# The head norm of a gated DeltaNet layer, computed inside the recurrence's stage with tokens on partitions

## The chip, the cores and the metric

The kernel runs as one program on one core of one Trainium2 chip. The metric is the device time of one execution in microseconds (us), smaller being better. The profiled execution gives, beside that time, a span: from the first to the last instruction that the profiler recorded. All times inside the kernel are counted from the start of the span. Engine names: PE is TensorE (matmuls), PEld its weight loads, DVE VectorE, ACT ScalarE, POOL GpSimd, SP SyncE, which issues the DMAs.

## What is computed

The reference is a stack of two transformer-like blocks over 16 + 512 tokens of width 1024. The change touches its first layer, a gated DeltaNet (GDN) with 16 value heads and 8 query/key heads of 128 features. Cut to what matters:

```python
def step(state, xs):                       # one chunk of tokens, all heads
    u_c, w_c, q_c, k_c, attn_c, last_c = xs
    v_new = u_c - einsum('bhck,bhkv->bhcv', w_c, state)
    o = einsum('bhck,bhkv->bhcv', q_c, state) + einsum('bhij,bhjv->bhiv', attn_c, v_new)
    state = state * last_c[..., None, None] + einsum('bhck,bhcv->bhkv', k_c, v_new)
    return state, o
...
def rms_norm(x, w):                        # over the 128 features of one head and token
    return x * lax.rsqrt(mean(x * x, axis=-1, keepdims=True) + 1e-6) * w
...
o = rms_norm(o, w_norm) * silu(z)          # the head norm, then the gate
return o.reshape(b, t, GDN_V_DIM) @ w_out  # 2048 -> 1024
```

## The kernel before

The program is a row of stages, each closed by a barrier over all engines. Four of them matter here. `gdn_front` projects the input and prepares the recurrence (up to about 356 us). `gdn_back` runs the recurrence (356 to 563.6 us). `head_norm` normalizes the 16 heads (563.6 to 589.7 us). `gated_down` (name `gdn_out`) gates the heads with silu(z) and multiplies by `w_out` (589.7 to about 703 us).

**gdn_back.** Its work is cut into 20 units, one for each of 5 chunks (16 tokens, then four of 128) and each of 4 groups of 4 heads. A hand-written order strings them into slots t = -1, 0, 1, ..., and every engine has its own function `step(t, real, level)` that lists what it does in slot t, for units at different distances: unit t+1 is prepared, unit t reads the old state, unit t-1 gets its new values, unit t-2 updates the state and gives its output, and unit t-3 is copied out. In slots 0 to 15 (`level`) the engines also build the inverse of a triangular matrix for unit t, blockwise: `turn5`, `open5`, `close5` on PE with `copy5` on ACT and `corner5` on DVE, then `open6`, `close6` with `copy6` and `corner6`. In slots 0 to 7 DVE has `second_half` besides: transposes of 32x32 blocks in slots 0, 1, 6 and 7 and 15 elimination steps in each of slots 2 to 5. The engines run their lists in order and meet at semaphores.

PE in slot t runs `turn5`, `old_values(t)`, `open5`, `new_values(t-1)`, `close5`, `prepare(t+1)`, `open6`, `update(t-2)`, `output(t-2)`, `close6`. All eight PSUM banks are in use, one for each purpose: `vb` holds the transposed values of `prepare`, `ob` the outputs. `output(u)` multiplies with features on PSUM's partitions (state or new values stationary, decayed queries or attention moving) and waits until `outputs(u-1)` on ACT has copied `ob` into the tile `wide` (`o_done`). `open6` waits for `corner5` (`y5_done`).

The chain that carries a slot to the next off PE goes from `differ(t+1)` on DVE (L1879) over a mask on POOL (L1658) and an exponential on ACT (L1803, `weights`) to `attention(t+1)` on DVE (L1868, L1873).

**head_norm.** For each of the 16 heads, 528 tokens wide: a square on POOL (L874), a sum over the features by a matmul with ones (L886), a logarithm and an exponential on ACT (L896, L903) and the product with gain on DVE (L916).

**gated_down.** ACT and DVE split the first two weight units into a high and a low part (`split_hi`, `split_lo`, L154 and L161), then each head: silu of z (L2055), product (L2079), high part (L2058), low part (L2074), and PE multiplies as soon as the low part is there. SP first issues the 1 MB weight unit that `gdn_back` has not loaded, then the z tiles, three ahead.

Of the kernel before, what the change touches and what calls it, by code (L numbers as in the profile page):

```python
# [16 lines left out]
F32 = mybir.dt.float32  # L17
# [131 lines left out]
def split_hi(k, act, u, slot, used):  # L149

    act.wait_ge(k.raw_landed[slot], landed_value(u, slot))
    if used is not None:
        act.wait_ge(k.tile_full, used)
    k.nc.scalar.copy(k.whi[:, slot % SPLIT_SLOTS, :], k.raw[:, slot, :]).then_inc(k.hi_done, 1)  # L154


def split_lo(k, eng, u, slot):

    eng.wait_ge(k.hi_done, u + 1)
    s = slot % SPLIT_SLOTS  # L160
    eng.tensor_tensor(k.wlo[:, s, :], k.raw[:, slot, :], k.whi[:, s, :].bitcast(F32),  # L161
                      ALU.subtract).then_inc(k.lo_done, 1)
# [37 lines left out]
def unit_tiles(k, pe, u, slot, kts, xhi, xlo, first_slot, tile_free, x_ready=None):  # L200
# [4 lines left out]
    whi = k.whi[:, s, :].rearrange("p (k n) -> p k n", k=kts)  # L205
    wlo = k.wlo[:, s, :].rearrange("p (k n) -> p k n", k=kts)
# [559 lines left out]
def weight_ring(k, name, ctx):  # L766
    sb = lambda nm, shape, dt: ctx.enter_context(k.nc.sbuf_tensor(f"{name}_{nm}", shape, dt))
    k.whi, k.wlo = sb("whi", [P, SPLIT_SLOTS, UNIT], F32R), sb("wlo", [P, SPLIT_SLOTS, UNIT], F32R)
# [74 lines left out]


def head_norm(k, name, n, tile, ones, scale, gain, gain_src=None, then=(), gain_parts=()):

    nc = k.nc
    with ExitStack() as ctx:  # L850
        sb = lambda nm, shape: ctx.enter_context(nc.sbuf_tensor(f"{name}_{nm}", shape, F32))
        sq, rinv = sb("sq", [P, 4, T]), sb("rinv", [P, 4, T])
        g = sb("g", [P, n])
        sem = lambda nm: k.sem(f"{name}_{nm}")
        gain_in, squared, summed, log, inv, done = (sem(x) for x in (
            "gain_in", "squared", "summed", "log", "inv", "done"))
        gain_set = sem("gain_set")
        past4 = lambda j: not (isinstance(j, int) and j < 4)
        block = ctx.enter_context(stage(k))

        @block.sync
        def _(sp):
            if gain_src is not None:
                with nc.allow_non_contiguous_dma(reason="gains, feature on partitions"):
                    sp.dma_start(g[:, 0:gain_src.shape[1]], gain_src).then_inc(gain_in, 16)
            if then:
                load_ahead(k, sp, k.unit, then)

        @block.gpsimd
        def _(pool):  # L870
            def square(j, b):
                if past4(j):
                    pool.wait_ge(summed, j - 3)
                pool.tensor_tensor(sq[:, b, k.now], tile(j)[:, k.now], tile(j)[:, k.now], ALU.mult).then_inc(squared, 1)  # L874
            for cols, value in gain_parts:
                pool.memset(g[:, cols], value).then_inc(gain_set, 1)
            rounds(pool, n, square, 4)

        @block.tensor
        def _(pe):  # L880
            def one(j, b):
                pe.wait_ge(squared, j + 1)
                if past4(j):
                    pe.wait_ge(log, j - 3)
                for hf, half in enumerate(k.halves):
                    mm = pe.matmul(k.ps[b][:, hf, 0:k.width], ones, sq[:, b, half], start=True, stop=True)  # L886
                mm.then_inc(summed, 1)
            rounds(pe, n, one, 4)

        @block.scalar  # L890
        def _(act):
            def logarithm(j, b):
                act.wait_ge(summed, j + 1)
                if past4(j):
                    act.wait_ge(done, j - 3)
                nc.scalar.activation(parted(k, rinv[:, b, k.now]), filled(k, k.ps[b]), ACT.Ln, scale=scale,  # L896
                                     bias=k.eps[:, :])\
                    .then_inc(log, 1)
            def one(j, b):
                if not (isinstance(j, int) and j == n - 1):  # L900
                    logarithm(j + 1, (b + 1) % 4)
                act.wait_ge(log, j + 1)
                nc.scalar.activation(rinv[:, b, k.now], rinv[:, b, k.now], ACT.Exp, scale=-0.5).then_inc(inv, 1)  # L903
            nc.scalar.preload_act_table_set("natural_log_exp_and_others")
            logarithm(0, 0)
            rounds(act, n, one, 4)

        @block.vector
        def _(dve):
            if gain_src is not None:  # L910
                dve.wait_ge(gain_in, 16)
            if gain_parts:
                dve.wait_ge(gain_set, len(gain_parts))
            def one(j, b):
                dve.wait_ge(inv, j + 1)
                dve.scalar_tensor_tensor(out=tile(j)[:, k.now], in0=tile(j)[:, k.now], scalar=gain(g, j),  # L916
                                         in1=rinv[:, b, k.now], op0=ALU.mult, op1=ALU.mult).then_inc(done, 1)
            rounds(dve, n, one, 4)
# [655 lines left out]
def gdn_back(k, g, qkv, an, d, tmp, yt, yt0, out_unit):  # L1574
# [13 lines left out]
    with ExitStack() as ctx:  # L1588
# [8 lines left out]
        x5, z5, xz6 = sb("x5", [P, GRP, CH]), sb("z5", [P, GRP * 64]), sb("xz6", [P, 2, GRP * 64])  # L1597
        v_in = [k.sem(f"gdns_v{j}") for j in range(VFS)]
        names = ("masks", "diffed", "lowered", "el_exp", "eq_exp", "dt_exp", "qd_done", "kd_done", "attn_done", "kq_ready",
                 "kt_ready", "kt_done", "vt_ready", "v_done", "ks_ready", "r_done", "new_ready", "new_done", "dec_done",  # L1600
                 "su_ready", "s_done", "o_ready", "o_done", "x5_ready", "x5_done", "z5_ready", "z5_done", "y5_ready",
# [14 lines left out]
        def slots(step):  # L1616
            for t in range(-1, nun + 3):
                step(t, lambda u: 0 <= u < nun, 0 <= t < NU)

        @block.sync  # L1620
        def _(sp):
# [45 lines left out]
        def _(pe):  # L1667
            key = lambda c, kh: qkv[:, GQ + kh, first_token(c):first_token(c) + size(c)]
            def prepare(u):
# [48 lines left out]
            def output(u):  # L1718
# [48 lines left out]
            def step(t, real, level):  # L1767
                if level:
# [21 lines left out]
        def _(act):  # L1790
            out = qkv[:, 0:2 * GQ, :].rearrange("p (o q) t -> p o q t", o=2)
# [51 lines left out]
            def step(t, real, level):  # L1843
# [4 lines left out]
                if real(t - 3):  # L1848
                    outputs(t - 3)
# [4 lines left out]
                if real(t + 1):  # L1854
                    values(t + 1)
                if level:
                    copy6(t)
                if t >= 0 and real(t + 1):
                    decays(t + 1)
            slots(step)  # L1860

        @block.vector
        def _(dve):
            def attention(u):
# [74 lines left out]
            def step(t, real, level):  # L1939
                if 1 <= t <= NU:  # L1940
                    corner6(t - 1)
                if t == -1:
                    differ(0)
                if real(t):
                    attention(t)
                if real(t - 3):
                    states(t - 3)
                if real(t):
                    residual(t)
                if real(t - 1):  # L1950
                    decayed(t - 1)
                if level:
                    corner5(t)
                second_half(t)
                if t >= 0 and real(t + 1):
                    differ(t + 1)
            slots(step)
# [21 lines left out]
def gdn(k, ins):  # L1979
# [3 lines left out]
    with ExitStack() as c:  # L1983
# [4 lines left out]
        with ExitStack() as c2:  # L1988
            split_rings(k, "gdn", c2)
            weight_ring(k, "gdnf", c2)  # L1990
# [4 lines left out]
        gdn_back(k, g, qk, an, d, tmp, yt, yt0, gdn_out_unit(ins))  # L1995


def gdn_out(k, ins, then):
    qk = k.wide[:, :].rearrange("p (j t) -> p j t", t=T)
    tile = lambda j: qk[:, bass.ds(j, 1), :].rearrange("p o t -> p (o t)")  # L2000
    head_norm(k, "gdn_on", GV, tile, k.ones[:, :], 1.0 / P, lambda g, j: g[:, 0:1],
              ins["gdn_norm"].rearrange("o p -> p o"))
    k.loaded = NCH - 1
# [5 lines left out]
def gated_down(k, name, cols, gate_d, value, acc, later_gains, then=()):  # L2009
# [7 lines left out]
    u0, t0, loaded = k.unit, k.tile, k.loaded  # L2017
    with ExitStack() as ctx:
# [30 lines left out]
        def _(act):  # L2049
            split_hi(k, act, u0, ring(0), t0)  # L2050
            split_hi(k, act, u0 + 1, ring(1), t0)
# [1687 lines left out]
```

## Time and profile before

| | us |
|---|---|
| median of 3 runs (range) | 2090.13 (2087.88 to 2090.97) |
| the profiled execution | 2084.21 |
| its span | 2082.5 |
| `gdn_back` | 356 to 563.6 |
| `head_norm` and its barrier | 563.6 to 589.7 |
| `gated_down`, until PE's first matmul | 589.7 to 599.4 |

The profiled execution is 5.9 us faster than the median of the others, so a sum that is made against its rows is added to the median for a forecast. A difference of 0.2% is 4.2 us.

### The profile page before, as it was taken

To read this page: it belongs to the slowest core of one execution; us is meant where nothing else is said; L and a number is where in the kernel's file an instruction comes from. 1 tells how busy PE (TensorE), PEld (TensorE's weight loads), DVE (VectorE), ACT (ScalarE), POOL (GpSimd) and SP (SyncE) were. 2 spreads that over 40 slices of the span, in tenths; PEclk is the share of its full clock that TensorE was granted. 3 is DMA by queue.
4 is the path that set the end of the run, shared out by engine and by line. 5 is a ranking of instruction groups with operands and counts; after the bars stand their busy time and mean duration, and the time that the engine had idled before them with its cause. 6 is when DMAs were issued, how large, how long until landed. Compare 5 with 4: busy or idle time off the path is not lost. (4 is left out here: it accounts for less than half of the span.)

```text
span 2082.5 us, 31710 instructions
## 1 busy us (share of the span) xinstructions
PE 1940.6 (93%) x12868; PEld 1735.1 (83%) x12868; DVE 1079.6 (52%) x1770; ACT 860.6 (41%) x1380; POOL 171.5 (8%) x190
## 2 busy tenths in 40 slices
PE   7999998999869999999989987899999998899988
PEld 6999998889769999999989965678888885787666
DVE  6657667675583344344444156544444447852243
ACT  6557742355572342233334244443332333424442
POOL 0001221022320000000000011000000002000101
PEclk9999999589989999999999999999999998999989
DMA  7223351113253222323223322223223222311101
GB/s 179 90 73 123 119 164 42 41 42 79 64 144 102 74 90 87 96 82 100 81 62 92 95 58 65 81 81 101 91 91 101 96 86 63 122 55 47 41 1 41
DMA packets 205246, 173.91 MB, mean 84 GB/s; under 512 B 41232, under 2 KB 180496, under 8 KB 205128
## 3 DMA queue, kind: packets, MB, share of 16 engines
q1 hardware_dynamic: 205128, 172.25, 27.9%
q8 instruction: 84, 1.38, 0.3%
q14 instruction: 34, 0.28, 0.0%
HBM read 161.40 MB, written 10.83 MB: 83 GB/s over the span
## 5 line engine op out<-in xcount | busy, mean ns | idle before, releaser
L161 DVE TENSOR_TENSOR main_wlo<-raw,main_whi 128x2048 fp32r<-128x2048 f32 x106 | 242.9, 2292 | 363.1 <-ACT main_whi L154 363.1
L154 ACT CAST main_whi<-raw 128x2048 fp32r<-128x2048 f32 x106 | 201.6, 1903 | 413.7 <-PE ps L176 412.4
L176 PE MATMUL ps<-ffn_xhi,main_whi 128*128 128x264 f32 (+1 forms) x768 | 205.3, 322 | 6.6 <-DVE ffn_xlo L646 6.6
L176 PE MATMUL ps<-ffn_xhi,main_wlo 128*128 128x264 f32 (+1 forms) x768 | 206.0, 323 | 0.0
L176 PE MATMUL ps<-ffn_xlo,main_whi 128*128 128x264 f32 (+1 forms) x768 | 205.8, 322 | 0.0
L176 PE MATMUL ps<-ffn_ahi,main_wlo 128*128 128x264 f32 (+1 forms) x768 | 205.4, 322 | 0.0
L176 PE MATMUL ps<-ffn_alo,main_whi 128*128 128x264 f32 (+1 forms) x768 | 205.2, 321 | 0.0
L176 PE MATMUL ps<-ffn_ahi,main_whi 128*128 128x264 f32 (+1 forms) x768 | 204.0, 320 | 0.0
L176 PE MATMUL ps<-gdn_xhi,gdnf_whi 128*128 128x264 f32 x768 | 162.2, 293 | 4.8 <-DVE gdn_xlo L517 4.4
L176 PE MATMUL ps<-gdn_xlo,gdnf_whi 128*128 128x264 f32 x768 | 158.3, 288 | 0.0
L176 PE MATMUL ps<-gdn_xhi,gdnf_wlo 128*128 128x264 f32 x768 | 158.1, 288 | 0.0
L176 PEld LDWEIGHTS ps<-ffn_xhi,main_whi 128*128 128x128 f32 x768 | 128.6, 189 | 18.9 <-issue 7.5
L176 PEld LDWEIGHTS ps<-ffn_ahi,main_whi 128*128 128x128 f32 x768 | 128.0, 189 | 11.6
L176 PEld LDWEIGHTS ps<-ffn_xhi,main_wlo 128*128 128x128 f32 x768 | 128.5, 190 | 10.9
L176 PEld LDWEIGHTS ps<-ffn_xlo,main_whi 128*128 128x128 f32 x768 | 127.7, 189 | 11.3 <-issue 0.2
L176 PEld LDWEIGHTS ps<-ffn_ahi,main_wlo 128*128 128x128 f32 x768 | 127.8, 189 | 10.9
L176 PEld LDWEIGHTS ps<-ffn_alo,main_whi 128*128 128x128 f32 x768 | 127.1, 188 | 11.1
L176 PEld LDWEIGHTS ps<-gdn_xhi,gdnf_whi 128*128 128x128 f32 x768 | 122.3, 191 | 6.5 <-issue 4.8
L359 DVE TENSOR_TENSOR h<-h,ps 128x528 f32<-128x528 f32 (+1 forms) x128 | 85.7, 692 | 80.2 <-PE ps L176 80.0
L176 PEld LDWEIGHTS ps<-gdn_xlo,gdnf_whi 128*128 128x128 f32 x768 | 120.9, 191 | 0.0
L176 PEld LDWEIGHTS ps<-gdn_xhi,gdnf_wlo 128*128 128x128 f32 x768 | 120.7, 191 | 0.0
L1158 DVE SCALAR_TENSOR_TENSOR gdnf_y<-gdnf_pre,gdnf_convw,gdnf_y 128x528 f32<-128x528 f32 x96 | 82.6, 862 | 61.6 <-ACT gdnf_y L1131 59.3
(473 smaller groups left out, 3851.7 us busy)
## 6 DMA issues: line engine op xcount, KB each, us to landing
raw<-in_ff_up_dram SPq DMA_DIRECT2D x32, 1024.0 KB, 5.4
raw<-in_ff_down_dram SPq DMA_DIRECT2D x32, 1024.0 KB, 5.0
raw<-in_gdn_in_dram SPq DMA_DIRECT2D x24, 1024.0 KB, 5.6
raw<-in_w_in_dram SPq DMA_DIRECT2D x14, 1024.0 KB, 5.3
raw<-in_mlstm_in_dram SPq DMA_DIRECT2D x12, 1024.0 KB, 5.4
raw<-in_gdn_out_dram SPq DMA_DIRECT2D x8, 1024.0 KB, 7.2
gdn_v_spilled<-gdnf_o SPq DMA_DIRECT2D x16, 264.0 KB, 2.2
gdn_z_spilled<-gdnf_o SPq DMA_DIRECT2D x16, 264.0 KB, 2.2
```

The lines of the kernel that those rows point to most:

```text
L154: k.nc.scalar.copy(k.whi[:, slot % SPLIT_SLOTS, :], k.raw[:, slot, :]).then_inc(k.hi_done, 1)
L161: eng.tensor_tensor(k.wlo[:, s, :], k.raw[:, slot, :], k.whi[:, s, :].bitcast(F32), ALU.subtract).then_inc(k.lo_done, 1)
L176: mm = pe.matmul(ps[:, b, 0:k.width], w, x[:, half], start=first and n == 0, stop=last and n == 2)
L359: dve.tensor_tensor(parted(k, acc[:, j, k.now]), parted(k, acc[:, j, k.now]), filled(k, k.ps[j % 4]), ALU.add).then_inc(s.down_free, 1)
L1158: dve.scalar_tensor_tensor(out=self.y[:, b, :], in0=self.pre[:, b, i:i + T], scalar=self.w[:, i, j:j + 1], in1=self.y[:, b, :], op0=ALU.mu ...
```

## The change

`head_norm` as a stage goes. Its work moves into `gdn_back`:

- `output(u)` swaps the operands of its matmuls, so that `ob` has tokens on partitions and features along the free axis.
- ACT squares `ob` (`square`, in the place of `outputs`), DVE sums over the features (`summed`), ACT takes logarithm and exponential of 4 numbers for each token (`root`) and writes the four heads scaled to a tile `hs` (`scale`). `root` and `scale` stand in the same slot, behind `values(t+1)` and ahead of `copy6`. The next unit's `output` waits for `scaled` in the place of `o_done`.
- One slot later PE turns the four heads by transposes (`back`) into the bank `vb`, at the head of its slot, and DVE multiplies by the gain and writes `wide` (`leave`). There is one slot more, t = 23.
- DVE takes `corner5(t)` ahead of `decayed(t-1)` and `residual(t)`.
- In slot 20 ACT and DVE split the first weight unit of `gated_down`, which does the second one alone. For this the weight ring is two separate tiles. `gated_down` issues three z tiles ahead of its 1 MB weight unit. The activation tables are loaded at the start and the end of `gdn_back`.
- SP issues one more small DMA (the gain) in `gdn_back`.

```diff
@@ gdn_back, PE
-                    pe.wait_ge(s.o_done, u)
+                    pe.wait_ge(s.scaled, GRP * u)
                 for h in range(GRP):
                     if c > 0:
-                        pe.matmul(ob[:, h, 0:n], st[:, GRP * i + h, :], eq[:, i, h, 0:n], start=True, stop=False)
-                    mm = pe.matmul(ob[:, h, 0:n], new[0:n, u % 2, h, :], dt[0:n, i, h, 0:n], start=c == 0, stop=True)
+                        pe.matmul(ob[0:n, h, :], eq[:, i, h, 0:n], st[:, GRP * i + h, :], start=True, stop=False)
+                    mm = pe.matmul(ob[0:n, h, :], dt[0:n, i, h, 0:n], new[0:n, u % 2, h, :], start=c == 0, stop=True)
                 mm.then_inc(s.o_ready, 1)
+            def back(u):
+                c, i = units[u]
+                n = size(c)
+                pe.wait_ge(s.scaled, GRP * (u + 1))
+                pe.wait_ge(s.v_done, GRP * min(u + 5, nun))
+                for h in range(GRP):
+                    mm = pe.transpose(vb[:, h, 0:n], hs[0:n, h, :], k.ident[0:n, 0:n])
+                mm.then_inc(s.h_turned, 1)
@@ gdn_back, ACT
-                nc.scalar.copy(out[:, :, 2 * i:2 * i + 2, t:t + n],
-                               ob[:, :, 0:n].rearrange("p (q o) n -> p o q n", o=2)).then_inc(s.o_done, 1)
+                if u >= 1:
+                    act.wait_ge(s.summed, u)
+                nc.scalar.square(sq[0:n, :, :], ob[0:n, :, :]).then_inc(s.squared, 1)
+            def root(u):
+                n, b = size(units[u][0]), u % 2
+                act.wait_ge(s.summed, u + 1)
+                nc.scalar.activation(var[0:n, b, :], var[0:n, b, :], ACT.Ln, scale=1.0 / CH, bias=k.eps[0:n, :])\
+                    .then_inc(s.log, 1)
+                act.wait_ge(s.log, u + 1)
+                nc.scalar.activation(var[0:n, b, :], var[0:n, b, :], ACT.Exp, scale=-0.5).then_inc(s.inv, 1)
+            def scale(u):
+                n = size(units[u][0])
+                act.wait_ge(s.inv, u + 1)
+                if u >= 1:
+                    act.wait_ge(s.h_turned, u)
+                for h in range(GRP):
+                    nc.scalar.activation(hs[0:n, h, :], ob[0:n, h, :], ACT.Copy, scale=var[0:n, u % 2, h:h + 1])\
+                        .then_inc(s.scaled, 1)
@@ gdn_back, DVE
+            def summed(u):
+                n = size(units[u][0])
+                dve.wait_ge(s.squared, u + 1)
+                dve.reduce_sum(var[0:n, u % 2, :].unsqueeze(2), sq[0:n, :, :], AX.X).then_inc(s.summed, 1)
+            def leave(u):
...
+                dve.wait_ge(s.h_turned, u + 1)
+                dve.tensor_scalar(out[:, :, 2 * i:2 * i + 2, t:t + n], vb[:, :, 0:n].rearrange("p (q o) n -> p o q n", o=2),
+                                  gain[:, 0:1], None, ALU.mult).then_inc(s.h_done, 1)
...
+                if real(t - 4):
+                    leave(t - 4)
                 if real(t):
                     attention(t)
                 if real(t - 3):
+                    summed(t - 3)
                     states(t - 3)
+                if level:
+                    corner5(t)
+                if real(t - 1):
+                    decayed(t - 1)
                 if real(t):
                     residual(t)
-                if real(t - 1):
-                    decayed(t - 1)
-                if level:
-                    corner5(t)
                 second_half(t)
                 if t >= 0 and real(t + 1):
                     differ(t + 1)
+                if t == nun:
+                    split_lo(k, dve, u_out, 0)
@@ gated_down, SP
-            for u in range(loaded, RAW_SLOTS):
-                load_unit(k, sp, u0 + u, cols(u), ring(u))
...
                 sp.dma_start(z[:, kt % 3, :], gate_d.ap()[kt]).then_inc(z_in[kt % 3], 16)
+                if kt == 2:
+                    for u in range(loaded, RAW_SLOTS):
+                        load_unit(k, sp, u0 + u, cols(u), ring(u))
```

How the instructions stand. First ACT, one full slot in the middle of `gdn_back` (slots 8 to 15 all read so), before:

```order
L1829 COPY wide<-ps 128x2x2x128
L1835 COPY gdns_x<-ps 96x4x96
L1837 COPY gdns_z<-ps 96x256
L1824 COPY gdns_new<-ps 128x512
L1810 COPY gdns_kt<-ps 128x256
L1816 ACTIVATE gdns_vt<-ps,gdn_beta 128x128 x4
L1842 COPY gdns_xz<-ps 64x512
```

The same place with the change (`gdns_sq` is the square, `gdns_var` the sums and their roots, `gdns_hs` the scaled heads):

```order
L1770 ACTIVATE gdns_sq<-ps 128x512
L1790 COPY gdns_x<-ps 96x4x96
L1792 COPY gdns_z<-ps 96x256
L1764 COPY gdns_new<-ps 128x512
L1750 COPY gdns_kt<-ps 128x256
L1756 ACTIVATE gdns_vt<-ps,gdn_beta 128x128 x4
L1774 ACTIVATE gdns_var<-gdns_var,eps 128x4
L1777 ACTIVATE gdns_var<-gdns_var 128x4
L1784 ACTIVATE gdns_hs<-ps,gdns_var 128x128 x4
L1797 COPY gdns_xz<-ps 64x512
```

The copy that frees `ob` was the slot's first, and what frees it now is L1784, ninth of ten. Next PE, from the end of one slot (`close6`) into the next (`turn5`, `old_values`), before:

```order
L1764 MATMUL ps<-gdns_xz 64x64 x4
L1737 MATMUL ps<-ident,raw 96x96 x4
L1694 MATMUL ps<-gdns_st,wide 128x128 x4
L1744 MATMUL ps<-raw,gdn_an 96x64 x4
L1706 MATMUL ps<-gdns_vt,raw 128x128 x4
```

and with the change:

```order
L1702 MATMUL ps<-gdns_xz 64x64 x4
L1667 MATMUL ps<-ident,gdns_hs 128x128 x4
L1675 MATMUL ps<-ident,raw 96x96 x4
L1624 MATMUL ps<-gdns_st,wide 128x128 x4
L1682 MATMUL ps<-raw,gdn_an 96x64 x4
L1636 MATMUL ps<-gdns_vt,raw 128x128 x4
```

Four transposes of 128x128 (L1667) stand at the head of each slot. Last DVE at the end of the stage, where the order of the last units decides (L1836 is `leave`, L1829 `summed`, L1884 `states`):

```order
L1836 TENSOR_SCALAR wide<-ps,gdns_gain 128x2x2x128
L1829 TENSOR_REDUCE gdns_var<-gdns_sq 128x4
L1884 SCALAR_TENSOR_TENSOR gdns_st<-gdns_st,gdns_el,ps 128x128 x4
L1836 TENSOR_SCALAR wide<-ps,gdns_gain 128x2x2x128
L1829 TENSOR_REDUCE gdns_var<-gdns_sq 128x4
L1884 SCALAR_TENSOR_TENSOR gdns_st<-gdns_st,gdns_el,ps 128x128 x4
L1836 TENSOR_SCALAR wide<-ps,gdns_gain 128x2x2x128
```

Before, only the state updates (L1910 there) stood in this place; a product and a reduction are now ahead of each.

## Rows read from the trace of the kernel before

**Rows 1.** The page: busy time, granted clock in 40 slices, the split's low part.

```profile
PE 1940.6 (93%) x12868; PEld 1735.1 (83%) x12868; DVE 1079.6 (52%) x1770; ACT 860.6 (41%) x1380; POOL 171.5 (8%) x190
PEclk9999999589989999999999999999999998999989
L161 DVE TENSOR_TENSOR main_wlo<-raw,main_whi 128x2048 fp32r<-128x2048 f32 x106 | 242.9, 2292 | 363.1 <-ACT main_whi L154 363.1
```

**Rows 2.** Busy time by stretch: us, each engine busy (count), granted clock, DMA share, GB/s.

```profile
459.00:526.50 67.50, 66.81 (x648) 62.62 (x647) 35.77 (x105) 38.15 (x94) 18.97 (x15) 1.00 0.37 87
526.50:563.60 37.10, 31.00 (x254) 29.87 (x253) 21.47 (x61) 15.58 (x36) 7.51 (x6) 0.95 0.21 58
549.60:553.00 3.40, 3.40 (x18) 3.40 (x18) 1.12 (x4) 0.00 (x0) 0.00 (x0) 0.51 0.00 0
563.60:589.70 26.10, 18.03 (x64) 10.85 (x64) 20.24 (x16) 20.66 (x33) 21.54 (x16) 1.00 0.00 0
```

**Rows 3.** Timeline of slot 10, PE: start, duration, instruction, [idle before <-releaser].

```profile
479.42 0.68 PE L1764 MATMUL ps<-gdns_xz 64*64 64x64 f32 x8
...
484.28 0.60 PE L1684 MATMUL ps<-ident,gdns_vf 128*128 128x128 f32 x4
...
484.98 0.25 PEld L1756 LDWEIGHTS ps<-ident,raw 64*64 64x64 f32 x4 [0.34 <-DVE raw L1917]
...
486.81 0.30 PEld L1728 LDWEIGHTS ps<-gdns_eq,gdns_st 128*128 128x128 f32 x2
...
488.80 0.68 PE L1764 MATMUL ps<-gdns_xz 64*64 64x64 f32 x8
```

**Rows 4.** The same slot on ACT.

```profile
484.92 1.14 ACT L1816 ACTIVATE gdns_vt<-ps,gdn_beta 128x128 f32<-128x128 f32 x4
...
486.03 0.58 ACT L1842 COPY gdns_xz<-ps 64x512 f32<-64x512 f32 x1
486.51 0.21 ACT L1796 ACTIVATE gdns_el<-gdns_eq 128x4 f32<-128x4 f32 x1
486.75 0.63 ACT L1798 ACTIVATE gdns_eq<-gdns_eq 128x512 f32<-128x512 f32 x1
```

**Rows 5.** Timeline of DVE in slots 4 and 17; a reduction elsewhere (busy, mean ns).

```profile
430.20 0.56 DVE L1868 COPY gdns_kd<-gdns_dt 128x4 f32<-128x4 f32 x1 [1.59 <-ACT gdns_dt L1803]
540.17 0.57 DVE L1868 COPY gdns_kd<-gdns_dt 128x4 f32<-128x4 f32 x1 [2.04 <-ACT gdns_dt L1803]
540.77 0.69 DVE L1873 TENSOR_TENSOR gdns_dt<-gdns_dt,ps 128x512 f32<-128x512 f32 x1
546.77 0.56 DVE L1868 COPY gdns_kd<-gdns_dt 128x4 f32<-128x4 f32 x1 [2.04 <-ACT gdns_dt L1803]
L3266 DVE TENSOR_REDUCE sm_var<-sm_ba 128x4 f32<-128x256 f32 x4 | 1.7, 419 | 5.0 <-ACT sm_ba L3132 5.0
```

**Rows 6.** Timeline from slot 16 on to the end of `gdn_back` and `head_norm`.

```profile
526.44 0.58 ACT L1829 COPY wide<-ps 128x512 f32<-128x512 f32 x1 [1.00 <-PE ps L1729]
549.24 1.65 PE L1716 MATMUL ps<-gdns_dec,gdns_kt 128*128 128x128 f32 x8 [1.89 <-DVE gdns_st L1910]
562.47 1.12 DVE L1910 SCALAR_TENSOR_TENSOR gdns_st<-gdns_st,gdns_el,ps 128x128 f32<-128x128 f32 x4 [3.17 <-PE ps L1729]
563.88 1.28 ACT L904 ACT_TABLE_LOAD   x1 [0.89 <-PEq L95]
587.95 1.45 DVE L916 SCALAR_TENSOR_TENSOR wide<-wide,gdn_on_g,gdn_on_rinv 128x528 f32<-128x528 f32 x2 [0.59 <-ACT gdn_on_rinv L903]
```

**Rows 7.** Timeline of the start of `gated_down`.

```profile
589.75 3.70 ACT L154 CAST main_whi<-raw 128x2048 fp32r<-128x2048 f32 x2 [1.30 <-PEq L95]
590.17 21.10 SPq L2039 DMA_DIRECT2D gdn_out_z<-gdn_z_spilled  x13
596.51 1.32 ACT L2055 ACTIVATE gdn_out_z<-gdn_out_z 128x528 f32<-128x528 f32 x2 [1.76 <-DMA gdn_out_z<-gdn_z_spilled]
599.45 0.78 PE L176 MATMUL ps<-gdn_out_ahi,main_whi 128*128 128x264 f32 x2 [12.80 <-DVE gdn_out_alo L2074]
```

More of the change, by code:

```diff
@@ L153, in split_hi @@
         act.wait_ge(k.tile_full, used)
-    k.nc.scalar.copy(k.whi[:, slot % SPLIT_SLOTS, :], k.raw[:, slot, :]).then_inc(k.hi_done, 1)
+    k.nc.scalar.copy(k.whi[slot % SPLIT_SLOTS][:, :], k.raw[:, slot, :]).then_inc(k.hi_done, 1)
 def split_lo(k, eng, u, slot):
@@ L160, in split_lo @@
     s = slot % SPLIT_SLOTS
-    eng.tensor_tensor(k.wlo[:, s, :], k.raw[:, slot, :], k.whi[:, s, :].bitcast(F32),
+    eng.tensor_tensor(k.wlo[s][:, :], k.raw[:, slot, :], k.whi[s][:, :].bitcast(F32),
                       ALU.subtract).then_inc(k.lo_done, 1)
@@ L842, in dve_end @@
         pass
[L845 to L918, printed above, removed]
@@ L1600, in gdn_back @@
                  "kt_ready", "kt_done", "vt_ready", "v_done", "ks_ready", "r_done", "new_ready", "new_done", "dec_done",
-                 "su_ready", "s_done", "o_ready", "o_done", "x5_ready", "x5_done", "z5_ready", "z5_done", "y5_ready",
+                 "su_ready", "s_done", "o_ready", "gain_in", "squared", "summed", "log", "inv", "scaled", "h_turned", "h_done", "x5_ready", "x5_done", "z5_ready", "z5_done", "y5_ready",
                  "y5_done", "xz6_ready", "xz6_done", "y6_ready", "y6_done", "cut", "stepped", "one", "back")
@@ L1616, in slots @@
         def slots(step):
-            for t in range(-1, nun + 3):
+            for t in range(-1, nun + 4):
                 step(t, lambda u: 0 <= u < nun, 0 <= t < NU)
@@ L1639, in _ @@
                     values(u)
+            with nc.allow_non_contiguous_dma(reason="128 gains, feature on partitions"):
+                sp.dma_start(gain[:, :], gain_col).then_inc(s.gain_in, 16)
             for t in range(nun):
@@ L1681, in prepare @@
                     pe.wait_ge(s.v_done, GRP * u)
+                if u >= 5:
+                    pe.wait_ge(s.h_done, u - 4)
                 pe.wait_ge(v_in[u % VFS], 16 * (u // VFS) + 16)
@@ L1767, in step @@
             def step(t, real, level):
+                if real(t - 4):
+                    back(t - 4)
                 if level:
@@ L1848, in step @@
                 if real(t - 3):
-                    outputs(t - 3)
+                    square(t - 3)
                 if level:
@@ L1855, in step @@
                     values(t + 1)
+                if real(t - 3):
+                    root(t - 3)
+                    scale(t - 3)
                 if level:
@@ L1859, in step @@
                     decays(t + 1)
+                if t == nun:
+                    split_hi(k, act, u_out, 0, None)
             slots(step)
+            nc.scalar.preload_act_table_set("silu_and_others")
         @block.vector
         def _(dve):
+            out = qkv[:, 0:2 * GQ, :].rearrange("p (o q) t -> p o q t", o=2)
+            def summed(u):
+                n = size(units[u][0])
+                dve.wait_ge(s.squared, u + 1)
+                dve.reduce_sum(var[0:n, u % 2, :].unsqueeze(2), sq[0:n, :, :], AX.X).then_inc(s.summed, 1)
+            def leave(u):
+                c, i = units[u]
+                n, t = size(c), first_token(c)
+                if u == 0:
+                    dve.wait_ge(s.gain_in, 16)
+                dve.wait_ge(s.h_turned, u + 1)
+                dve.tensor_scalar(out[:, :, 2 * i:2 * i + 2, t:t + n], vb[:, :, 0:n].rearrange("p (q o) n -> p o q n", o=2),
+                                  gain[:, 0:1], None, ALU.mult).then_inc(s.h_done, 1)
             def attention(u):
@@ L1994, in gdn @@
                       tiles, UnitHeads(g, qk), blocks, an)
-        gdn_back(k, g, qk, an, d, tmp, yt, yt0, gdn_out_unit(ins))
+        gdn_back(k, g, qk, an, d, tmp, yt, yt0, ins["gdn_norm"].rearrange("o p -> p o"), gdn_out_unit(ins))
 def gdn_out(k, ins, then):
     qk = k.wide[:, :].rearrange("p (j t) -> p j t", t=T)
[L2000 to L2003, printed above, removed]
+    k.loaded, k.split = NCH - 1, 1
     o = lambda kt: qk[:, (kt % 2) * GQ + kt // 2, :]
@@ L2016, in gated_down @@
     n, kts = KD, GV
-    u0, t0, loaded = k.unit, k.tile, k.loaded
+    u0, t0, loaded, split = k.unit, k.tile, k.loaded, k.split
     with ExitStack() as ctx:
@@ L2049, in _ @@
         def _(act):
-            split_hi(k, act, u0, ring(0), t0)
-            split_hi(k, act, u0 + 1, ring(1), t0)
+            for u in range(split, 2):
+                split_hi(k, act, u0 + u, ring(u), t0)
             for kt in range(kts + 1):
@@ L2069, in _ @@
         def _(dve):
-            split_lo(k, dve, u0, ring(0))
-            split_lo(k, dve, u0 + 1, ring(1))
+            for u in range(split, 2):
+                split_lo(k, dve, u0 + u, ring(u))
             def low(kt):
```

47 lines of the change are left out of this document (25 added, 22 removed).

## The prediction

> **What bounds the kernel now.** Start with the page [rows 1]: PE is busy for 93% of the span and VectorE for 52%, and the line of the granted clock has two low places, at the start of `gdn_back` and around 590 us. So the kernel is bound by PE wherever PE has work, and what the change touches is a stretch where it has little or none. The table by stretch [rows 2] shows this. From 459 to 526.5 us PE is busy for 66.81 of 67.50 us: these are the slots in which the recurrence and the inverse run side by side, and PE's list is the limit. From 526.5 to 563.6 us it is busy for 31.0 of 37.1 us, and chains between engines are the limit. In `head_norm`, 563.6 to 589.7 us, PE's 18.03 us are only sums by ones: the stage runs at the pace of POOL (21.54 us for 16 squares). Then `gated_down` starts with 9.7 us in which PE has nothing [rows 7].
>
> **What goes.** The last instruction of `gdn_back` ends at 562.47 + 1.12 = 563.59 [rows 6] and `gated_down` starts at 589.75 [rows 7]. Between lie `head_norm` and two barriers. One barrier stays; it costs 563.88 - 563.59 = 0.3 us [rows 6]. Saved: 589.75 - 563.59 - 0.3 = **25.9 us**. All of it is on the path, since no engine has anything else there.
>
> **The start of `gated_down`.** Before, ACT splits two units (3.70 us), and the first z tile is there only at 596.51, 6.76 us after the stage's start, because 1 MB of weights was issued ahead of it [rows 7]. From silu to PE's first matmul it takes 599.45 - 596.51 = 2.94 us. Now ACT splits one unit (half of 3.70, 1.85 us), DVE its low part (2.29 us, rows 1), so DVE is free at 4.2 us. The z tiles go first: at the old rate three tiles of 264 KB and the 1 MB unit, 1.86 MB, took 590.17 to 596.51; the first tile should be there at 2.5 to 3.5 us. So DVE's split is last, and PE starts at about 4.2 + 2.94 - 0.67 (the silu is done by then) = 6.4 us in place of 9.7. Saved: **3.3 us**; bounds 2 (z comes late) and 4.1. The fourth z tile now comes behind the weights, about 1 us late, and PE, whose clock is at half after the pause, hides that.
>
> **A slot in the middle (slots 8 to 15).** The slot lasts 488.80 - 479.42 = 9.38 us from `close6` to `close6` [rows 3], and PE idles in it only before `open6` (0.34 us of the weight loader, waiting for `corner5`). The wait for `ob` costs nothing: its copy is ACT's first act. With the change, `output` waits for `scale`, and `scale` stands behind `values(t+1)`. I follow the chain:
> - `close6` to the transposes of the values: 484.28 - 479.42 = 4.86.
> - The new transposes of `back`: four of the kind of L1684; the cycle there is about 0.11 each, 0.45.
> - Transposes to ACT's `values`: 484.92 - 484.28 = 0.64. Four products: 486.03 - 484.92 = 1.11 [rows 4].
> - Logarithm and exponential of four numbers: by the step from L1796 to L1798, 0.24 each, 0.48 [rows 4].
> - `scale`: four scaled copies from PSUM of 128x128, exactly the form of L1816, 1.14. Signal to PE 0.05.
> - `output` up to `close6`: 488.80 - 486.81 = 1.99 [rows 3].
>
> Sum 10.72, so +1.34 per slot, and PE stands for about 1.0 us ahead of `output`. The earlier `corner5` removes the 0.34 at `open6`, but this is not a gain any more: PE gets to the wait for `scale` sooner. Eight slots: **+10.7 us**. Square (for the copy, both one pass over 128x512) and DVE's two additions are beside this chain: DVE has 35.77 busy us in 67.50 [rows 2]. What the numbers leave open here is small, since all parts have rows: 9 to 12 us.
>
> **The early slots.** In slots 2 to 7 DVE's eliminations and transposes make the slot. `leave` falls into DVE's wait for the decays (1.59 us in slot 4, rows 5) and costs nothing. `summed` does not. A reduction of 128x256 takes 0.42 us [rows 5]; for twice the elements I take 0.65, near the 0.69 of a pass over 128x512. Slots 3 to 7: 5 x 0.65 = **+3.3 us**; bounds 1.5 and 5.
>
> **The late slots and the end.** Before, from the end of `output(13)` (its copy starts at 526.44) to 563.59 it takes 37.15 us [rows 6]. With the change:
> - Slot 16, the chain above without `open5`, `close5`, `turn5`, `open6`: 9.1.
> - Slots 17 and 18: before 546.77 - 540.17 = 6.60, the loop `differ`, POOL, ACT, `attention` [rows 5]. Now the loop over `ob` is longer: `back` 0.45, two products of 8 instructions (`output` has 16 in 1.99, so some 0.93 each), `prepare` with 10 instructions and its signal 1.36, `values` 1.11, root 0.48, `scale` 1.19, `output` 1.99 = 8.5 each.
> - `output(17)`: `back` and its signal 0.65, `leave` 0.6, L1868 0.56, L1873 0.6, reduction 0.6, states 1.07, update 0.9, output 1.99 = 7.0. `output(18)`, without the two of `attention`: 5.8.
> - `output(19)`: ACT splits the weight unit (1.9) once `scale(17)` is done, DVE its low part (2.29) behind that, and only then `leave(17)`, the sum and the states of 18. DVE gets free 2.2 us after `output(18)`: 2.2 + 0.6 + 0.65 + 1.07 + 0.9 + 1.99 = 7.4.
> - After it: square 0.6, sum 0.65, root 0.48, `scale` 1.14, `back` 0.65, `leave` 0.65, signals 0.7 = 4.9, where before it was states alone, 1.2.
>
> Sum 9.1 + 17.0 + 7.0 + 5.8 + 7.4 + 4.9 = 51.2. The clock: before, after a pause of 1.89 us the granted clock was 0.51 from 549.6 to 553.0 (1.2 GHz in place of 2.4, rows 2), and update and output took longer: L1716 1.65 us [rows 6]. Half the clock over 3.4 us costs PE **1.7 us** where it is on the path. PE now pauses over 3 us ahead of `output(19)`, so I add one fall, 1.7. Together 52.9 - 37.15 = **+15.8 us**; bounds 12 (no fall, short reduction) and 20 (a fall in each late slot too).
>
> The two table loads, 1.28 us each [rows 6], lie beside other work: the first beside the DMAs that start the stage, the last beside `back` and `leave` of unit 19. The Trainium skill ("ScalarE: Activation LUTs", What ACT_TABLE_LOAD costs) adds a drain of about 1.38 us to each load, which speaks against the change, as the last load would end behind `leave`: by it the time would be about 1.4 us longer. The row shows only the load, and the sum goes by the row.
>
> **The sum.** Against the profiled execution: -25.9 - 3.3 + 10.7 + 3.3 + 15.8 = +0.6 us, so 2084.8 where 2084.21 was. Added to the median 2090.13: **2091 us**. The stage that goes is paid back nearly in full by a longer wait for one PSUM bank.
>
> **The rivals.**
> *The clock falls in the waits (slower).* Each middle slot gets a pause of 1.0 us, each of slots 16 to 18 one of about 1.6. In rows 2 the clock held at 1.00 with pauses of 0.34, and fell to 0.51 after the one of 1.89; between them no row shown decides. If it falls in five of those eleven slots, it costs 5 x 1.7 = 8.5 us: 2099. From three falls on (5.1 us) the change is measurably slower. The Trainium skill ("TensorE: Matmul & The Clock Gate", HAM oscillation) says that a loop which waits between its groups of matmuls can drop to the lower clock in every turn; `head_norm` in rows 2, with PE busy for 18.03 of 26.10 us at clock 1.00, speaks against it. Chance 0.25, and 0.05 for slower by other means, above all more DVE time in the early slots.
> *The terms all fall to the cheap side (faster).* No fall of the clock at the end (-1.7), `summed` hidden in most early slots (-2), z early (-0.8), late slots a little shorter (-1): about 2085. Chance 0.13.
> *The wait for `ob` isn't last (faster).* If `values` and `scale` ran early enough, a middle slot would cost only the 0.45 of `back` less the 0.34 at `open6`, and the change would gain 8 x 1.2 + 4 in the late slots: 2077. Against it speak rows 3 and 4: `values` waits for PE's transposes at 484.92 and `output` began at 486.81, so 1.67 us of new ACT work can't fit between. Chance 0.07.
> *The change doesn't do what it says:* the earlier `corner5` gains nothing. This I expect, as told above; it is part of the forecast.
>
> **How the numbers follow.** Forecast 2091 with chance 0.5; its own range is 2087 to 2095. The range for 8 in 10 reaches from 2085 (the cheap sides) to 2101 (five to six falls, with the dearer early slots). Measurements of this kernel can tell 0.2%, 4.2 us, from no change: faster 0.2, same 0.5, slower 0.3.
>
> **What would show it.** In the new profile: (1) `gated_down` follows `gdn_back` by 0.3 us. (2) Middle slots of 10.7 us, with PE idle for about 1 us ahead of L1658, released by ACT L1784; no idle at L1694. (3) Slots 17 and 18 near 8.5. (4) DVE's split (2.29) behind `scale(17)`, and `output(19)` late by it. (5) PE's first matmul of `gated_down` at 6.4 us. (6) A clock below 0.9 between 459 and 560 us would be the first rival. I am wrong by most if the middle slot is not 10.7: each 0.1 us is 0.8 us of the time.

## The result, and the profile after

Over 20 runs each, the changed kernel takes 2093.11 us in the median (2085.29 to 2097.01) and the kernel before 2088.63; the ratio of the means is 1.0020, 95% interval 1.0011 to 1.0029. So it is slower by 4.2 us (2.3 to 6.1): the interval leaves out 1, but the difference itself lies at the 0.2% that was taken ahead of the result as the bound of what can be told. One execution of the kernel before (6515.53 us) and one of a kernel below, with the bank copied away and DVE's old order (5560.24 us), were slow ones and are in no ratio. The profiled execution took 2089.14 us (span 2087.4), against 2084.21.

Busy time by stretch of the changed kernel (us, each engine busy (count), granted clock, DMA share, GB/s): the middle slots, where PE was busy for 66.81 us [rows 2], then slots 17 and 18 (outputs 15 and 16), and the place where the clock fell.

```profile
459.00:526.50 67.50, 61.39 (x583) 57.11 (x583) 41.97 (x112) 42.23 (x118) 15.66 (x13) 1.00 0.26 64
551.89:560.28 8.39, 6.60 (x56) 6.18 (x55) 5.37 (x14) 5.59 (x16) 2.49 (x3) 1.00 0.14 31
560.28:568.79 8.51, 6.61 (x56) 6.19 (x55) 5.37 (x14) 5.59 (x17) 2.54 (x3) 1.00 0.60 157
585.50:589.00 3.50, 3.43 (x17) 3.46 (x18) 0.00 (x0) 0.64 (x3) 0.00 (x0) 0.52 0.00 0
```

Timeline of slot 10 on ACT and PE (start, duration, instruction, [idle before <-releaser]); these answer [rows 3] and [rows 4].

```profile
477.96 0.60 ACT L1770 ACTIVATE gdns_sq<-ps 128x512 f32<-128x512 f32 x1 [0.46 <-PE ps L1659]
...
483.81 1.15 ACT L1756 ACTIVATE gdns_vt<-ps,gdn_beta 128x128 f32<-128x128 f32 x4
484.82 0.31 ACT L1774 ACTIVATE gdns_var<-gdns_var,eps 128x4 f32<-128x4 f32 x1
485.17 0.20 ACT L1777 ACTIVATE gdns_var<-gdns_var 128x4 f32<-128x4 f32 x1
485.41 1.14 ACT L1784 ACTIVATE gdns_hs<-ps,gdns_var 128x128 f32<-128x128 f32 x4
...
486.70 0.46 PE L1658 MATMUL ps<-gdns_st,gdns_eq 128*128 128x128 f32 x2 [0.89 <-ACT gdns_hs L1784]
...
488.76 0.60 ACT L1770 ACTIVATE gdns_sq<-ps 128x512 f32<-128x512 f32 x1 [0.46 <-PE ps L1659]
```

The square, first reader of `ob`, comes every 10.80 us, where the copy came every 9.38. PE stands for 0.89 us until `scale`'s fourth copy frees the bank; ACT goes from `values` through the root to `scale` without a pause.

The end of `gdn_back`, on all engines; these answer [rows 6] and [rows 7].

```profile
578.90 1.91 ACT L154 CAST main_whi<-raw 128x2048 fp32r<-128x2048 f32 x1
580.85 2.29 DVE L161 TENSOR_TENSOR main_wlo<-raw,main_whi 128x2048 fp32r<-128x2048 f32 x1 [1.94 <-ACT main_whi L154]
583.06 0.74 DVE L1836 TENSOR_SCALAR wide<-ps,gdns_gain 128x512 f32<-128x512 f32 x1
583.72 0.68 DVE L1829 TENSOR_REDUCE gdns_var<-gdns_sq 128x4 f32<-128x512 f32 x1
584.31 1.11 DVE L1884 SCALAR_TENSOR_TENSOR gdns_st<-gdns_st,gdns_el,ps 128x128 f32<-128x128 f32 x4
585.57 2.05 PE L1646 MATMUL ps<-gdns_dec,gdns_kt 128*128 128x128 f32 x8 [3.76 <-DVE gdns_st L1884]
593.63 1.28 ACT L1821 ACT_TABLE_LOAD   x1
594.36 0.75 DVE L1836 TENSOR_SCALAR wide<-ps,gdns_gain 128x512 f32<-128x512 f32 x1 [1.46 <-PE ps L1667]
595.46 1.90 ACT L154 CAST main_whi<-raw 128x2048 fp32r<-128x2048 f32 x1 [0.55 <-PEq L95]
599.10 1.33 ACT L2032 ACTIVATE gdn_out_z<-gdn_out_z 128x528 f32<-128x528 f32 x2 [1.74 <-DMA gdn_out_z<-gdn_z_spilled]
602.03 0.78 PE L176 MATMUL ps<-gdn_out_ahi,main_whi 128*128 128x264 f32 x2 [7.71 <-DVE gdn_out_alo L2051]
```

`split_lo` stands in DVE's list ahead of `leave`, the sum and the states that PE's next update needs: PE pauses for 3.76 us, and the update takes 2.05 us at clock 0.52, where the one of the unit before took 1.13. `gdn_back` ends at 594.36 + 0.75 = 595.11, and the next stage follows by 595.46 - 595.11 = 0.35 us.

### The profile page after: what moved, and what is told of

Its sections match the earlier page's. It is cut to its first block and busy times, and to the rows that moved or that the text cites. A ratio compares the mean times of both kernels' runs of the same rounds, so it can differ in the third digit from the quotient of the medians.

```text
span 2087.4 us, 31791 instructions
## 1 busy us (share of the span) xinstructions
PE 1935.4 (93%) x12884; PEld 1728.9 (83%) x12884; DVE 1079.9 (52%) x1794; ACT 872.2 (42%) x1468; POOL 150.2 (7%) x174
## 3 DMA queue, kind: packets, MB, share of 16 engines
q8 instruction: 84, 1.38, 0.3%
## 5 line engine op out<-in xcount | busy, mean ns | idle before, releaser
L161 DVE TENSOR_TENSOR main_wlo<-raw,main_whi 128x2048 fp32r<-128x2048 f32 x118 | 271.1, 2297 | 373.8 <-ACT main_whi L154 373.8
L154 ACT CAST main_whi<-raw 128x2048 fp32r<-128x2048 f32 x118 | 224.5, 1903 | 409.9 <-PE ps L176 409.4
L349 DVE TENSOR_TENSOR ffn_alo<-wide,ffn_ahi 128x528 fp32r<-128x528 f32 (+1 forms) x64 | 44.8, 700 | 87.9 <-ACT ffn_ahi L307 87.9
L442 ACT ACTIVATE wide<-wide 128x528 f32<-128x528 f32 (+1 forms) x64 | 40.9, 639 | 106.9 <-DVE wide L449 106.9
L176 PE MATMUL ps<-gdn_xhi,main_whi 128*128 128x264 f32 x384 | 81.4, 294 | 4.4 <-DVE gdn_xlo L517 4.4
L176 PE MATMUL ps<-mls_xhi,main_whi 128*128 128x264 f32 (+1 forms) x320 | 80.4, 317 | 5.0 <-DVE mls_xlo L517 4.3
L176 PE MATMUL ps<-gdn_xhi,gdnf_whi 128*128 128x264 f32 x384 | 80.1, 290 | 2.5 <-DVE gdnf_wlo L161 2.5
L176 PE MATMUL ps<-sec_xhi,main_whi 128*128 128x512 f32 x176 | 75.9, 431 | 5.6 <-DVE sec_xlo L517 4.4
```

The source lines that it names most:

```text
L154: k.nc.scalar.copy(k.whi[slot % SPLIT_SLOTS][:, :], k.raw[:, slot, :]).then_inc(k.hi_done, 1)
L161: eng.tensor_tensor(k.wlo[s][:, :], k.raw[:, slot, :], k.whi[s][:, :].bitcast(F32), ALU.subtract).then_inc(k.lo_done, 1)
L176: mm = pe.matmul(ps[:, b, 0:k.width], w, x[:, half], start=first and n == 0, stop=last and n == 2)
L349: dve.tensor_tensor(alo[:, par, m, k.now], k.a[:, m % 2, k.now], ahi[:, par, m, k.now].bitcast(F32), ALU.subtract).then_inc(s.lo, 1)
L442: k.nc.scalar.square(k.a[:, m % 2, k.now], k.b[:, m % 2, k.now]).then_inc(s.a_ready, 1)
```

## Experiments

Below, a slot is measured from one read of `ob` by ACT to the next, and output(u) stands for the read that follows unit u's output. Each ratio is to the kernel before, with its 95% interval.

**The bank copied away.** ACT copies `ob` to SBUF ahead of its square; `scale` reads the copy, and `output` waits for copy and square, not for `scale`. One kernel has this alone, one also has DVE's old order (residual, decayed, corner). The diff is cut to what matters: the lines stand in PE's `output`, ACT's `square` and ACT's `scale`.

```diff
-                    pe.wait_ge(s.scaled, GRP * u)
+                    pe.wait_ge(s.o_done, 2 * u)
...
+                    act.wait_ge(s.scaled, GRP * u)
-                nc.scalar.square(sq[0:n, :, :], ob[0:n, :, :]).then_inc(s.squared, 1)
+                nc.scalar.copy(oc[0:n, :, :], ob[0:n, :, :]).then_inc(s.o_done, 1)
+                nc.scalar.square(sq[0:n, :, :], ob[0:n, :, :]).then_inc(s.o_done, 1)
...
-                    nc.scalar.activation(hs[0:n, h, :], ob[0:n, h, :], ACT.Copy, ...)
+                    nc.scalar.activation(hs[0:n, h, :], oc[0:n, h, :], ACT.Copy, ...)
```

> The change with one thing altered: ACT first copies the output bank to SBUF and squares it, output(u+1) waits for these two only, and scale reads the copy. ACT gets 0.58 us more work in each slot. Theory A (the added time in the recurrence is the wait for scale on one PSUM bank): the middle slot falls from 10.80 to 9.6 us (9.38 + 0.45 for the transposes - 0.25 of the wait at open6), the idle time of PE ahead of output goes, slots 17 and 18 fall from 8.4 to about 7.4, the early waits for scale go; in all 12 to 15 us less than the change, so about 2079, faster than before by 0.4%. Theory B (the added work on ACT, DVE and PE as such fills the slots): middle slots stay at 10.8 or grow, since ACT has more to do; 2093 or more.

Measured: 2076.56 us, 0.9965 (0.9952 to 0.9977). Four middle slots by stretch, then two of PE's operations, `open6` and the first of `output`, neither with a wait ahead of it:

```profile
477.90:516.58 38.68, 38.68 (x379) 36.63 (x378) 25.78 (x68) 28.80 (x81) 10.18 (x9) 1.00 0.35 83
```
```profile
492.13 0.41 PE L1695 MATMUL ps<-ident,raw 64*64 64x64 f32 x4
...
494.07 0.39 PE L1659 MATMUL ps<-gdns_st,gdns_eq 128*128 128x128 f32 x2
```

A slot is 38.68 / 4 = 9.67 us and PE is busy for all of it. So the bank's wait costs 10.80 - 9.67 = 1.13 us a slot. The other 9.67 - 9.38 = 0.29 us is PE's own list.

> As x_copy, but VectorE takes residual, decayed values and then corner5, in the old order. If the earlier corner is worth something only where PE does not wait for scale anyway: middle slots 0.25 us longer than in x_copy (the 0.34 of idle weight loader ahead of open6 is back), so 2 to 3 us slower than x_copy. If DVE's order does not matter: the same.

Measured: 2084.45 us, 0.9989 (0.9976 to 1.0002). Against 0.9965 with the new order that is 5 us slower by the ratios, and 8 by the medians, where I expected 2 to 3. Four slots by stretch, then DVE and PE in slot 11:

```profile
479.86:521.82 41.96, 38.95 (x378) 36.62 (x376) 25.43 (x68) 29.71 (x82) 10.15 (x9) 1.00 0.32 76
```
```profile
494.15 1.12 DVE L1867 SCALAR_TENSOR_TENSOR gdns_vt<-ps,gdn_tok,gdns_vt 128x128 f32<-128x128 f32 x4
495.19 0.68 DVE L1875 TENSOR_TENSOR gdns_dec<-ps,gdns_kd 128x512 f32<-128x512 f32 x1
495.79 0.59 DVE L1894 COPY raw<-ps 32x128 f32<-32x128 f32 x2
496.43 0.41 PE L1695 MATMUL ps<-ident,raw 64*64 64x64 f32 x4 [0.75 <-DVE raw L1894]
```

DVE works without a pause from `leave` and the sum (0.75 + 0.68 us, new with the change) to the corner, and PE waits for the corner behind residual and decayed: 10.49 us a slot, 0.82 more. The order of the corner is worth this much here, where the bank is not last.

**The corner's order alone**, in the changed kernel and in the kernel before (three calls in another order).

> The change, but VectorE in the old order (residual, decayed, corner5). The prediction said that the earlier corner gains nothing here, since PE then stands for scale: middle slots stay 10.80, PE idles at open6 for about 0.3 us and correspondingly less ahead of output; the time within 1 us of the change. The rival: the corner is worth 0.3 us in a slot, 8 to 16 slots, 3 to 5 us slower than the change.

Measured: 2087.99 us, 1.0015 (1.0003 to 1.0027), middle slots 10.79: as the changed kernel. PE's waits between 470 and 530 us, of this kernel and then of the changed one (total, times, longest):

```profile
PE ps L1694 <- DVE raw L1891: 4.5, 6, 0.8
```
```profile
PE ps L1658 <- ACT gdns_hs L1784: 5.4, 6, 0.9
```

With either order PE has one wait in a slot and the slot is as long: the wait only moves from one place to the other.

> The kernel before with one part of the change alone: DVE takes the corner ahead of decayed and residual. In the kernel before PE stands for 0.34 us of each middle slot ahead of L1756 for this corner. Theory A: the wait goes, a middle slot goes from 9.38 to 9.04, eight slots give 2.7; in slots 3 and 4, at PE's low clock, DVE now stands ahead of the corner with residual behind it, as in the changed kernel (waits of 3.4 and 2.5 us), which costs 1 to 2 back. Net about 1 us faster. Theory B: residual or decayed is late instead, PE waits at L1716, and the slot stays at 9.38.

Measured: 2087.14 us, 1.0005 (0.9993 to 1.0016). Middle slots 9.21, half of the expected gain, with no wait of PE left in them: 9.21 is PE's list. Of the weight loader's 0.34 us of idle only 0.17 counted for the slot. And 9.67 - 9.21 = 0.46 is what PE's new work costs, which is the four transposes of `back` (0.45 by the forecast). The gain doesn't reach the total: the slots up to output(6) took 3.7 us longer than in the kernel before (75.30 against 71.61 us from output(0) on).

**The root taken away**, to see whether PE follows ACT's chain. The kernel leaves out the logarithm and the exponential, and its output is not the norm.

```diff
-                nc.scalar.activation(var[0:n, b, :], var[0:n, b, :], ACT.Ln, ...)
-                nc.scalar.activation(var[0:n, b, :], var[0:n, b, :], ACT.Exp, scale=-0.5)
```

> The changed kernel without the logarithm and the exponential of the four sums per unit: that part of the head norm is left out, and ACT scales by the raw sum. They take 0.31 and 0.20 us on ACT between `values` and `scale`, and scale(u) starts 0.59 us after them in the changed kernel. Theory A (PE waits at L1658 for the chain transposes, values, root, scale): a middle slot goes from 10.80 to 10.21, PE's pause from 0.89 to 0.3; eight slots and the four late units give 12 x 0.59 = 7 us, so about 0.997 of the changed kernel and at or a little under the kernel before. Theory B (the slot is set by the extra work on PE and DVE, and the wait only shows it): a slot moves by under 0.1 us and the time by under 1 us.

Measured: 2081.44 us, 0.9981 (0.9972 to 0.9990); middle slots 10.23, PE's pause:

```profile
484.99 0.46 PE L1658 MATMUL ps<-gdns_st,gdns_eq 128*128 128x128 f32 x2 [0.32 <-ACT gdns_hs L1779]
```

0.57 us off the chain gave 0.57 us of every middle slot: theory A. The chain is what ends last.

**The sum made short** (`sq[0:n, :, 0:16]`; the kernel leaves out seven eighths of the sum).

> The changed kernel with DVE's sum over 16 in place of 128 squares a head (the rest of the sum is left out), so L1829 takes about 0.15 in place of 0.68 us. My prediction put 0.65 us of each of five early slots on this sum. If it is on DVE's path there, the time from output(1) to output(6) falls from 61.6 to about 59.0; a middle slot stays at 10.80, because DVE isn't what PE waits for there; units 16 to 19 and the end gain 5 x 0.5 = 2.5. Together about 5 us. The rival for the early slots (PE's waits and its low clock make them, not DVE's extra work): they stay at 61 or more, and only the 2.5 us of the end are gained.

Measured: 2090.72 us, 1.0025 (1.0013 to 1.0037): nothing gained. From output(1) to output(6) it took 60.87 us, against 61.60 and, in the second profile of the changed kernel, 61.63. So the sum accounts for about 0.7 us there and not for 3.3; this is one profile, and others of the same instructions differ by more (point 5 below). In slots 17 and 18 the clock fell, and they took 9.20 and 9.82 us in place of 8.39 and 8.51. From output(16) to the next stage it took 595.95 - 570.85 = 25.1 us in place of 26.7, which is the gain at the end that I had expected, in part.

**The split, the z tiles, and the changed kernel once more.** One kernel makes both of the stage's first splits in `gated_down`; one issues the z tiles behind the weights, as before the change; one is unaltered.

> The changed kernel with no weight unit split inside `gdn_back`; `gated_down` splits two units at its start, as before the change. If DVE's split (1.9 us of waiting for ACT's part, and 2.29) is what makes output(19) late, PE's pause of 3.76 us ahead of L1646 goes down to 1.5 or less, the fall of the clock there too, and the time from output(18) to output(19) falls from 8.7 to about 6. The first matmul of `gated_down` comes at about 9 us of that stage in place of 6.57. The two nearly cancel: within 1 us of the changed kernel. If the split is harmless where it stands, the back stage is unchanged and the time is 2.5 us longer.

Measured: 2090.79 us, 1.0020 (1.0009 to 1.0032), as the changed kernel. PE's pause ahead of the last update was shorter, if not as short as I expected, and the update ran at the full clock:

```profile
586.98 1.13 PE L1646 MATMUL ps<-gdns_dec,gdns_kt 128*128 128x128 f32 x8 [2.56 <-DVE gdns_st L1882]
```

Output(18) to output(19) took 5.91 us in place of 8.68, and PE's first matmul came 603.91 - 595.31 = 8.6 us into the stage, behind DVE's two splits. But slots 17 and 18, whose instructions are those of the changed kernel, were slower:

```profile
551.23:560.96 9.73, 7.94 (x56) 7.52 (x55) 5.38 (x14) 5.59 (x16) 2.54 (x3) 0.85 0.09 27
560.96:571.01 10.05, 8.15 (x56) 7.73 (x55) 5.37 (x14) 5.59 (x17) 2.50 (x2) 0.84 0.59 133
```

> The changed kernel once more, unaltered. In two kernels whose instructions are those of the changed kernel up to the split or but for a shorter sum, PE's clock fell in units 15 and 16, after pauses of 1.5 to 2.1 us, and those two slots took 9.2 to 10.05 us in place of 8.39 and 8.51; and output(0) to output(3) took 42.5 or 46.2 us with the clock at 0.75 or at 0.50 in the second slot. If both are chance, where the clock falls differs from one profile to the next, and this one may show either: early part 42 to 46.5, late slots 8.4 or 9.7 to 10. If the kernel's code sets it, this profile repeats the first: 46.2 in the early part and 8.4 and 8.5 late. Middle slots are 10.80 in either case.

Measured: 2090.95 us, 1.0018 (1.0006 to 1.0031). Slots 17 and 18 of this profile:

```profile
552.22:561.83 9.61, 7.82 (x56) 7.41 (x55) 5.37 (x14) 5.58 (x17) 2.54 (x3) 0.86 0.09 27
561.83:570.74 8.91, 7.01 (x56) 6.60 (x55) 5.37 (x14) 5.58 (x17) 2.49 (x2) 0.96 0.57 150
```

The same kernel, with the clock at 1.00 there in one profile and at 0.86 in the other, after the same pause (1.45 and 1.44 us ahead of L1658 in slot 17): the code alone doesn't decide. The early part (46.2 us from output(0) to output(3)) repeated the first profile.

> The changed kernel with `gated_down`'s z tiles issued behind the 1 MB weight unit, as before the change. The first z then comes about 6.8 us after the stage's start in place of 3.6, and it, not DVE's split, is last: PE's first matmul at 9.7 in place of 6.57 us, so about 3 us slower than the changed kernel. If DVE's split is last anyway, the first matmul stays near 6.6 and the order of the DMAs gains nothing.

Measured: 2095.03 us, 1.0037 (1.0023 to 1.0051), 4 us slower than the unaltered kernel beside it. PE's first matmul came at 609.80 - 600.25 = 9.55 us, against 6.40 in the unaltered one. The order of the DMAs gives 3.2 us, but not alone: with the z tiles first and two splits in the stage it was 8.6.

**A version that beats both.** To the copied bank comes another order of the end: from slot 20 on DVE does the states ahead of the sum and of `leave`, and its split comes two slots later. Cut from the diff are the lines that take sum and `leave` out of their old places there, and a wait of `back` for `leave`.

```diff
+                if late:
+                    if real(t - 3):
+                        summed(t - 3)
+                    leave(t - 4)
...
-                if t == nun:
+                if t == nun + 2:
                     split_lo(k, dve, u_out, 0)
```

> As x_copy; besides, from slot 20 on VectorE updates the states before it sums and before it writes the turned heads, and splits the weight unit in slot 22 in place of 20. If the end of the stage is held up by VectorE's order (output(18), output(19) wait for the states behind leave, sum and split): the stretch from output(16) to the stage's end is shorter by 1.3 us for each of two outputs and about 2 us for the split, 4 us less than x_copy. If the ends of the chain are on ACT, nothing changes.

Measured: 2073.48 us, 0.9945 (0.9929 to 0.9960). From output(13) to the next stage it took 578.54 - 533.64 = 44.9 us, against 49.1 with the copied bank alone and 52.7 in the changed kernel, a gain of 4 us as expected.

> The copied-bank kernel with its end reordered (states ahead of the sum and the turned heads, split two slots later), and in slots 2 to 4 DVE's old order again: residual, decayed, then the corner. In those slots PE's clock is at half and the corner comes late, so that DVE with the corner first stood for 2.47 and 3.41 us ahead of it, with residual behind; in the changed kernel with the old order throughout, output(0) to output(2) took 30.9 in place of 32.6 us. So about 1.5 us faster than the same kernel without this (2073.5), that is 2072. If those slots are set by PE's low clock instead, the time is the same within 0.5 us.

Measured: 2072.39 us, 0.9936 (0.9921 to 0.9950). Output(0) to output(6) took 76.75 us against 77.1, where I expected 1.5 us less. The intervals of the two kernels overlap for the most part, so no effect of the old order in the first slots is shown.

## The prediction, point by point

The time lies in the range (2093.1 within 2085 to 2101), and the main mechanism was right: the stage that goes is paid back, for the most part by the wait for the bank and by the end of the stage. The forecast itself, no measurable change (+0.6 us by its sum), was 3.6 us too low. That 2091 looks closer to 2093.1 than this is luck: its base, 2090.13, came from three runs, and 20 runs gave 2088.63. From PE's first transposes in `gdn_back` (356.80 us before, 356.12 after) to its first matmul in `gated_down` it took 242.65 us before, and 245.91 and 248.91 in the two profiles of the changed kernel, so +3.3 and +6.3 where the sum had +0.6. Most of this difference is in point 5, and in the second profile in point 6 and the last update as well (output(18) to output(19) took 9.65 us in it, 8.68 in the first). In the first profile another 2.3 us lie behind that matmul, where the profiles of all kernels here differ by 6 us (1481.6 to 1487.7), so no cause is given for them.

1. *The stage that goes*: 25.8 us, predicted 25.9. *The start of `gated_down`*: first matmul at 6.57 us, predicted 6.4. It takes both parts, the z tiles first (9.55 without) and one split in place of two (8.6 without).
2. *Middle slots*: 10.80 us, predicted 10.72, by the chain I followed, with the pause where I put it (0.89 us, predicted about 1.0). Removing 0.57 us of the chain removed as much from the slot, and freeing the bank 1.13.
3. *The earlier corner*: nothing in the middle slots here, as predicted. Its price of 0.34 was misread (the weight loader's idle, of which 0.17 counted), and that it would be worth 0.82 with the bank free was not seen.
4. *Late slots and end*: from output(13) on +15.2 us, predicted +15.8, with slots of 8.39 and 8.51 (predicted 8.5), the split ahead of unit 17's `leave`, and one fall of the clock.
5. *Early slots*: this term was mis-sized, and its reason was wrong. I put in 3.3 us, all of it for the sum, and 1.34 for the middle slot that ends with output(6): 4.6. From PE's first transposes in `gdn_back` to output(6) it took 103.96 us before and 111.04 after: 7.1, beyond my upper bound too. The slot that ends with output(6) even got shorter, from 8.56 to 8.36 us. I had said that DVE's eliminations make these slots. But from output(0) to output(6) before, DVE was busy for 52.94 of 71.61 us and PE for 67.71; after, DVE for 57.60 of 78.04 and PE for 72.20. (The wait of 1.59 us that I gave to slot 4 is also one of slot 6.) The sum is about 0.7 us of it. Five waits of PE for `scale`, 3.6 us together, are new there, and the sum had no term for them; but with the bank copied away, where they are gone, the same stretch took 77.11 us, so they alone don't explain it either. Where the clock is low matters as well, slot 4 before, in the changed kernel and in the one without the split:

```profile
404.99:418.79 13.80, 12.66 (x98) 11.51 (x97) 10.93 (x27) 4.84 (x14) 2.50 (x3) 0.75 0.25 67
405.56:421.70 16.14, 16.14 (x87) 13.38 (x86) 11.57 (x29) 6.69 (x20) 2.49 (x3) 0.50 0.13 34
407.64:421.24 13.60, 12.56 (x93) 10.68 (x93) 11.49 (x29) 6.59 (x20) 2.50 (x3) 0.75 0.17 40
```

The last two have the same instructions. From output(0) to output(6) four profiles with these instructions took 78.04, 78.06, 75.33 and 76.76 us, where it was 71.61 before. The corner's new order alone, put into the kernel before, gave 14.41 us at 0.50 for slot 4 and 75.30 in all. So these slots cost 3.7 to 6.5 us. What sets the place of the low clock stays open, and so does how much of the rest comes from the corner's order, since the changed kernel with the old order was no faster there (78.28).
6. *The rival of the falling clock*: refuted for the middle slots (clock 1.00 from 459 to 526.5, with a pause of 0.89 in each), but not for slots 16 to 18, whose pauses ahead of L1658 are 1.44 to 1.55 us. Of four profiles with these instructions one shows the clock at 1.00 in slots 17 and 18; in the other three it fell, and slots 16 to 18 together took 1.6 to 4.7 us longer. I gave the rival as all or nothing; this part of it, and point 5, are what the forecast lacked. The kernel with two splits in `gated_down` also shows the clock at 1.00 after one pause of 2.56 us, so the length of a single pause doesn't decide either.

The drain that the Trainium skill ("ScalarE: Activation LUTs", What ACT_TABLE_LOAD costs) adds to a table load isn't seen: the last load ends at 593.63 + 1.28 = 594.91, and ACT's next instruction starts 0.55 us later, with the barrier as its releaser. By the Trainium skill's figure it would have been 1.38 us later at least. Ahead of the load there is no room for it either: `scale` ends at 592.47 + 1.14 = 593.61.

## What to carry to other kernels

A stage that is folded into a loop takes its time back through whatever it holds there: here a PSUM bank, kept over one pass of ACT's list. Copying the bank away cost ACT 0.57 us a slot that it had to spare, and turned 4 us lost into 7 gained (11 and 13 in the two kernels with the end reordered). An order of instructions may be worth nothing while another wait is last, and 0.82 us a slot when that wait is gone, so try such parts again after each repair.

## What I had not expected of the hardware

With 0.89 us of pause in each 10.80 us slot, PE's clock stayed at 1.00 for 67.5 us. With 1.44 to 1.55 us (and 0.35 at another place) in each of slots 16 to 18, it held in one profile and fell to 0.86 in the next, of the same kernel. Two instructions of 128x4 on ACT cost 0.57 us together, nearly as much as one pass over 128x512.
